# A decoder step's mixing tile in another order: an inverse without transpositions, its last level by substitution, and the next tile's scores and routing rows inside it

## What is computed

```python
A = jnp.where(strict, jnp.einsum('bhncd,bhnjd->bhncj', kb, k) * decay, 0.0)
sol = lax.linalg.triangular_solve(eye + A, rhs, left_side=True, lower=True, unit_diagonal=True)
u, w = sol[..., :dv], sol[..., dv:]
qk = jnp.where(causal, jnp.einsum('bhncd,bhnjd->bhncj', q, k) * decay, 0.0)
...
    v_new = u_c - jnp.einsum('bhcd,bhde->bhce', w_c, S)
    o = jnp.einsum('bhcd,bhde->bhce', qg_c, S) + jnp.einsum('bhcj,bhje->bhce', qk_c, v_new)
    S = S * gl_c[..., None, None] + jnp.einsum('bhcd,bhce->bhde', kd_c, v_new)
```

## Time and profile before

| | us |
|---|---|
| median of 3 runs | 1625.16 (1621.95 to 1626.21) |
| the profiled execution | 1621.55 |
| its span, first to last instruction | 1619.7 |
| the mixing stage in it | 578.4 (406.6 to 985.0) |
| PE busy in the mixing stage | 528.5 |
| DVE, ACT, POOL busy in it | 405.6, 300.5, 109.7 |
| one tile, from o products to o products | 69.5 (742.9 to 812.4) |

### The profile page before, as it was taken

The page is one execution under the profiler, slowest core; times in us unless marked ns, Lnnn a source line. Parts: engine busy times, 40 slices in busy tenths (PEclk is TensorE's granted clock), DMA queues, the critical chain, the costliest instruction groups (busy, mean ns, idle before and its releaser), DMA issues. The chain is left out here.

```text
span 1619.7 us, 24144 instructions
## 1 busy us (share of the span) xinstructions
PE 1405.5 (87%) x9708; PEld 955.3 (59%) x9708; DVE 625.8 (39%) x1034; ACT 349.4 (22%) x730; POOL 215.9 (13%) x284
## 2 busy tenths in 40 slices
PE   6999999604899999999899983699999999839997
PEld 4679999502577686776868652445454545414443
DVE  2325452107554646546364525312121212124442
ACT  2322322101323323233232310011111111111111
POOL 0000000001302113021221200122222121100000
PEclk9999999855988988898887976799999999969999
DMA  5212322243202112021120106489999999633320
GB/s 178 85 40 79 104 85 86 27 143 103 83 8 76 40 44 82 8 76 31 54 82 9 40 4 240 164 307 348 339 352 338 360 342 341 243 126 110 111 71 27
DMA packets 149127, 218.03 MB, mean 135 GB/s; under 512 B 12476, under 2 KB 123652, under 8 KB 144423
## 3 DMA queue, kind: packets, MB, share of 16 engines
q1 hardware_dynamic: 130862, 168.92, 31.3%
q0 software_dynamic: 9504, 25.77, 4.2%
q10 hardware_dynamic: 8681, 22.14, 3.8%
HBM read 178.91 MB, written 42.54 MB: 137 GB/s over the span
## 5 line engine op out<-in xcount | busy, mean ns | idle before, releaser
L1719 PE MATMUL psum<-experts 128*128 128x512 f32 x528 | 235.2, 599 | 2.6 <-DVE experts L1741 2.6
L626 PE MATMUL psum<-split_parts 128*128 128x344 f32 x1224 | 194.1, 321 | 0.0
L626 PEld LDWEIGHTS psum<-split_parts 128*128 128x128 f32 x1224 | 193.9, 188 | 0.1
L1719 PEld LDWEIGHTS psum<-experts 128*128 128x128 f32 x528 | 101.2, 192 | 130.4 <-issue 127.2
L2094 PE MATMUL psum<-experts 128*128 128x512 f32 x288 | 127.5, 601 | 3.9 <-DVE experts L2005 3.9
L1735 PE MATMUL psum<-experts 128*128 128x512 f32 x264 | 119.2, 594 | 1.5 <-ACTq L1772 1.0
L1756 DVE COPY experts<-psum 128x256 f32<-128x256 f32 x33 | 14.0, 425 | 274.9 <-PE psum L1726 274.9
L1304 PE MATMUL psum<-decode_and_mix 128*128 128x512 f32 x256 | 114.9, 603 | 0.7 <-ACT decode_and_mix L1227 0.7
L1021 POOL TENSOR_TENSOR decode_and_mix<-decode_and_mix,lasting 128x16 f32<-128x16 f32 (+3 forms) x25 | 44.7, 1786 | 423.5 <-DVE decode_and_mix L1077 241.8
L2094 PEld LDWEIGHTS psum<-experts 128*128 128x128 f32 x288 | 55.6, 193 | 74.2 <-issue 69.9
L1304 PEld LDWEIGHTS psum<-decode_and_mix 128*128 128x128 f32 x256 | 48.2, 193 | 56.6 <-issue 55.2
(11 more groups left out here) (369 smaller groups left out, 1978.4 us busy)
## 6 DMA issues: line engine op xcount, KB each, us to landing
experts<-in_w_gate SPq DMA_DIRECT2D x33, 1024.0 KB, 5.9
experts<-in_w_up SPq DMA_DIRECT2D x33, 1024.0 KB, 10.7
experts<-in_w_down SPq DMA_DIRECT2D x33, 1024.0 KB, 12.3
project<-in_w_in SPq DMA_DIRECT2D x18, 512.0 KB, 4.9
experts<-ye_d SPq DMA_DIRECT2D x16, 512.0 KB, 5.3
conv_out_d<-project ACTq DMA_DIRECT2D x12, 512.0 KB, 3.1
decode_and_mix<-conv_out_d SPq DMA_DIRECT2D x8, 768.0 KB, 4.7
until_mixed<-in_x_prompt SPq DMA_DIRECT2D x8, 512.0 KB, 4.7
```

The source lines that it names most:

```text
L626: mm = nc.tensor.matmul(thirds(u)[:, b], w[:, u, k, :], x[:, k, b * TB:(b + 1) * TB], start=(i == 0 and k == 0), stop=(i == 2 and k == KD ...
L1719: mm = nc.tensor.matmul(bank(2 + s.v), xgT[s.v][:, k, :], wgu[s.u][:, k, :], start=(k == 0), stop=(k == KD - 1))
```

## The change

The tile is put into another order on all engines.

- The inverse no longer turns MT at each level. PE keeps M, the transpose of MT, summed up in PSUM: `added_product` adds was' Xs to it, beside PT = Xs' was for MT, and the masks of levels 1 to 5 carry the sign (so DVE adds). A level is X, then PT and M for each group; ACT copies X and M.
- The sixth level is gone. v of the low half is formed with the low inverse, w = ATo' vn is taken off the high half's right side (DVE), then v of the high half: `quarter` products of 64x64. ATo is multiplied by E_ and not by Eb.
- The next tile's scores stand in levels 4 and 5, and their bias, maximum and shift in DVE's level 4 and after level 5; its exponentials stand on ACT ahead of and after `squared`. The gates' sums and the turning of the next tile's tokens follow dS. The turning of the residual rows stands in level 3, and the router's product in two halves between v low, w and v high. The second half of the projection is cut in three, between the turnings, G, QK and values.
- POOL multiplies Eb and the output gate by its gain (szn), and makes gU for the next tile early. Masking of the first tile's scores is done for it alone. pT has two buffers, and PSUM banks are dealt out anew. All engines' loops over tiles are written out. The SBUF room of the stages (WORDS) grows from 50400 to 53200 words.

Core of the diff: SP, POOL, DVE, ACT and PE in turn; lines that begin with - of the old order are left out, except in two places.

```diff
-        c[:, C_LV + n * HD:C_LV + (n + 1) * HD] = (row // (2 * s) == near // (2 * s)) & (row // s < near // s)
+        c[:, C_LV + n * HD:C_LV + (n + 1) * HD] = ((row // (2 * s) == near // (2 * s)) & (row // s < near // s)) * (-1.0 if n else 1.0)
...
+                for t in range(NT):
+                    if t:
                         sp.wait_ge(S("tokv_ps"), t)
                         settle(sp)
+                        load_conv(sp, t * P)
                         sp.wait_ge(S("av_ps"), t)
+                        load_attention(sp, t, t * P)
+                    load_out(t)
+                    sp.wait_ge(S("szn"), t)
+                    sp.dma_start(szst, sz_d[t * P:(t + 1) * P, :]).then_inc(S("sz_in"), 16)
+                load_out(NT)
...
+                gates(0)
+                for t in range(NT):
+                    R = DEC if t == 0 else P
+                    if t:
                         rms_pow("o", r8, m8, NH, t - 1)
                     rms_pow("qk", r16, m16, 16, t)
+                    g.wait_ge(S("E"), t + 1)
+                    g.tensor_tensor(Eb, E_, bc(gb[:, t, 0:NH], P), ALU.mult).then_inc(S("Eb"), 1)
+                    if t < NT - 1:
+                        gates(t + 1)
+                    g.wait_ge(S("AT"), 3 * t + 2)
+                    for l in range(1, 4):
+                        masked(t, l)
                     rms_pow("x", rsx[0:R], msx[0:R], 1, t)
+                    for l in range(4, LV):
+                        masked(t, l)
+                    g.wait_ge(S("sz_in"), 16 * t + 16)
+                    if t:
+                        g.wait_ge(S("v_on"), t)
+                    g.tensor_tensor(slots(szn), natural(szst), slots(bm(normB, NH)), ALU.mult).then_inc(S("szn"), 1)
...
                 def gated_out(t):
                     v.wait_ge(S("r_o"), t + 1)
-                    V.tensor_tensor(o_, o_, bc(r8, HD), ALU.mult).then_inc(S("v_on"), 1)
                     v.wait_ge(S("v_on"), t + 1)
-                    V.tensor_tensor(natural(vn.rearrange("p h d -> p (h d)")), slots(o_), slots(r_), ALU.mult).then_inc(S("og"), 1)
...
+                    for l in range(1, LV):
                         for g in range(2):
...
+                            v.wait_ge(S(f"PT{g}_ps"), (LV - 1) * t + l)
+                            V.tensor_tensor(MT[l % 2][:, hs], MT[(l - 1) % 2][:, hs], PT_ps(g), ALU.add).then_inc(S(f"MT{g}"), 1)
+                        if l == 1:
+                            mean_square(t, R)
...
                             V.tensor_tensor(r_, vtok, tmp, ALU.subtract).then_inc(S("r"), 1)
+                        if l == 2:
+                            normed(t, R)
+                            V.tensor_tensor(slots(tmq), kqS_ps[:, :, 1], slots(bc(egam, HD)), ALU.mult).then_inc(S("v_qS"), 1)
...
+                        if l == 3:
+                            gain(t, R)
+                        if l == 4 and more:
+                            biased(t + 1, 0)
+                            maximum(t + 1, 0)
+                            shift(t + 1, 0)
+                    if more:
+                        biased(t + 1, 1)
+                        maximum(t + 1, 1)
                     for g in range(2):
...
+                        v.wait_ge(S(f"v{g}_ps"), 2 * t + 1)
+                        V.tensor_tensor(vn[LOW, hs], v_ps(g)[LOW], bc(gb[LOW, t, hs], HD), ALU.mult).then_inc(S(f"vn{g}"), 1)
+                    if more:
+                        shift(t + 1, 1)
+                    v.wait_ge(S("r"), t + 1)
+                    for g in range(2):
...
+                        v.wait_ge(S(f"w{g}_ps"), t + 1)
+                        V.tensor_tensor(r_[HIGH, hs], r_[HIGH, hs], w_ps(g)[HIGH], ALU.subtract).then_inc(S(f"r1{g}"), 1)
+                    logits(t, R)
+                    for g in range(2):
...
+                        v.wait_ge(S(f"v{g}_ps"), 2 * t + 2)
+                        V.tensor_tensor(vn[HIGH, hs], v_ps(g)[HIGH], bc(gb[HIGH, t, hs], HD), ALU.mult).then_inc(S(f"vn{g}"), 1)
...
+                def tile(t):
+                    R, more = DEC if t == 0 else P, t < NT - 1
+                    act.wait_ge(S("tok_ps"), t + 1)
+                    A.activation(sq, tok_ps, ACT.Square).then_inc(S("sq"), 1)
+                    act.wait_ge(S("tokv_ps"), t + 1)
+                    act.wait_ge(S("r"), t)
+                    A.activation(slots(vtok), natural(tokv_ps), ACT.Copy).then_inc(S("vtok"), 1)
+                    if t:
                         mix_rows(t - 1)
...
+                    for l in range(LV):
+                        if l > 0:
...
+                                act.wait_ge(S(f"X{g}_ps"), (LV - 1) * t + l)
+                                A.activation(Xs[:, 4 * g:4 * g + 4], X_ps(g), ACT.Copy).then_inc(S(f"X{g}"), 1)
+                        if l < LV - 1:
...
+                                act.wait_ge(S(f"M{g}_ps"), (LV - 1) * t + l + 1)
+                                A.activation(M_[:, 4 * g:4 * g + 4], M_ps(g), ACT.Copy).then_inc(S(f"M{g}"), 1)
+                        if l == 0:
+                            norm_rows(t, R)
+                        if l == 3:
+                            store_rows(t, R)
+                    if more:
+                        exps(t + 1, 0)
+                    squared(t)
+                    if more:
+                        exps(t + 1, 1)
...
+                def added_product(out, g, left, right, first=False):
+                    for h in range(4 * g, 4 * g + 4):
+                        for rows in (LOW, HIGH):
+                            mm = T.matmul(out[rows, h % 4, :], left(rows, h), right(rows, h), start=first and h == 4 * g, stop=True, skip_group_check=True)
+                    return mm
...
+                def quarter(out, g, left, right):
+                    for h in range(4 * g, 4 * g + 4):
+                        mm = T.matmul(out[:, h % 4, :], left[:, h, :], right[:, h, :], start=True, stop=True)
+                    return mm
...
+                def tile(t):
+                    R, more = DEC if t == 0 else P, t < NT - 1
+                    if t:
                         turn_out(t - 1)
                         pe.wait_ge(S("mixB"), t)
+                        pe.wait_ge(S("mixA"), t)
...
+                    else:
+                        pe.wait_ge(S("s1"), 2)
...
+                    project(t, 0, range(KD))
                     pe.wait_ge(S("qk"), t + 1)
                     pe.wait_ge(S("D"), t + 1)
                     pe.wait_ge(S("egam"), t + 1)
...
+                    turned_weights(t, 0)
+                    project(t, 1, range(5))
                     pe.wait_ge(S("qkT"), t + 1)
...
+                        mm = T.matmul(G_ps[:, s, :], kT, kT, start=True, stop=True)
                     mm.then_inc(S("G_ps"), 1)
...
+                    turned_weights(t, 1)
+                    pe.wait_ge(S("pT0"), t + 1)
...
+                        mm = T.matmul(QK_ps[:, s, :], qkT[half_of(h), 4 + h // 2, :], qkT[half_of(h), h // 2, :], start=True, stop=True)
                     mm.then_inc(S("QK_ps"), 1)
+                    project(t, 1, range(5, 6))
                     pe.wait_ge(S("pT1"), t + 1)
+                    values(t, 0)
+                    values(t, 1).then_inc(S("av_ps"), 1)
+                    project(t, 1, range(6, KD)).then_inc(S("proj_ps"), 1)
+                    for g in range(2):
+                        pe.wait_ge(S(f"MT{g}"), LV * t + 1)
+                        if g == 1:
                             pe.wait_ge(S("mixA"), t + 1)
+                        added_product(M_ps(g), g, lambda rows, h: MT[0][rows, h, :], lambda rows, h: ident[rows, rows], first=True).then_inc(S(f"M{g}_ps"), 1)
+                    for l in range(1, LV):
+                        was = MT[(l - 1) % 2]
+                        for g in range(2):
+                            pe.wait_ge(S(f"M{g}"), (LV - 1) * t + l)
+                            pe.wait_ge(S("Lo"), (LV - 1) * t + l)
+                            pe.wait_ge(S("AT"), 3 * t + 3)
+                            pe.wait_ge(S(f"MT{g}"), LV * t + l)
+                            inverse_product(X_ps(g), g, lambda rows, h: Lo[l][rows, h, :], lambda rows, h: M_[rows, h, :]).then_inc(S(f"X{g}_ps"), 1)
+                        if l == 1:
+                            pe.wait_ge(S("QK"), t + 1)
...
+                            mm.then_inc(S("kS_ps"), 1)
+                        if l == 3:
+                            turn_rows(t, R)
+                        if l == 4 and more:
+                            scores(t + 1, 0)
+                        if l == 5 and more:
+                            scores(t + 1, 1)
+                        for g in range(2):
+                            pe.wait_ge(S(f"X{g}"), (LV - 1) * t + l)
+                            pe.wait_ge(S(f"MT{g}"), LV * t + l)
+                            inverse_product(PT_ps(g), g, lambda rows, h: Xs[rows, h, :], lambda rows, h: was[rows, h, :]).then_inc(S(f"PT{g}_ps"), 1)
```

(21 more changed lines are left out.)

506 lines of the change are left out of this document (217 added, 289 removed).

## The result

The changed kernel takes **1580.5 us** (median of 4 runs, 1579.27 to 1584.67) against 1624.34 (4 runs): a ratio of 0.9735, 95% interval 0.9712 to 0.9758. That is 43.8 us faster; 27.4 were forecast. The time lies in the stated range of 1564 to 1621, but under the 1584 to 1612 that the forecast had as its own. In the profiled executions the span went from 1619.7 to 1577.2 us, 42.5 less.

What follows compares the result with a forecast made beforehand. A tile was bound by PE's queue plus its waits. Six tiles 22.8, last 7.1, first -3.2, end 0.7: 27.4 us off 1621.55 gives 1594.2, plus 3.6 to the median: 1598; range 1564 to 1621, its own 1584 to 1612.

Steps and rivals of the forecast that it cites:

- full clock throughout: Rival: routing between the quarters keeps the clock up; tile 60.0 us, whole kernel 1562 us; chance 0.17.
- S1: Tile from end of o to the projection: the chain, not PE, sets it; 7.9 us before and after.
- S2: Tile from projection to inverse: 25.8 us before, 21.5 summed at full clock, 22.4 with the low clock.
- S3: Tile from the inverse to level 5: levels of 3.0 against 3.54 us; 24.9 before, 22.1 summed, 22.2 in the tile.
- S4: Tile's tail, last level, v and o: 10.9 us before, 9.2 at full clock, 12.2 forecast with the low stretch.
- Clock: Whole tile: order alone worth 3.5 us, the rest clock; 60.0 at full clock, 64.7 with the remaining low stretch.
- first low stretch: Clock at 0.50 in the old tile's inverse, 777.9 to 784.7; should go with the wait ahead of it.
- second stretch: Clock at 0.50 from 805.2 into the next tile's scores; should stay, since one-quadrant products with waits remain.
- First tile, last tile, end: Mixing stage's edges: first tile 67.3 against 64.1 us, last tile 7.1 less, 0.7 less after it.
- Into the projection: Rival: the low stretch runs on through S1 into the projection, +2.6 us a tile, 1618 us; chance 0.10.
- DVE late: Rival: DVE late ahead of MT or vn, waits longer than summed, +2 us a tile, 1613 us; chance 0.10.
- The inverse at 1.2 GHz: Rival: the inverse's products run at half clock, 9.5 us more a tile, 1671 us; chance 0.08.

Runs made afterwards that it cites:

- dve_late2: Changed kernel, with VectorE forming vn of the low half before the next tile's bias and maximum, and logits in their own bank: 1566.5 us.
- order: Changed kernel with vn before bias and maximum (logits in own bank), gated output ahead of E_, and first tile's exponentials behind its square: 1556.3 us.
- order_sd: The order kernel with the next tile's second scores moved into the tail and two 512-column products that nothing reads: 1565.3 us.

## Why the prediction was right, and by how much it was off

The time fell into the range, and the named mechanism holds: the new order shortens PE's queue, the low stretch ahead of the inverse goes and the one at the o products stays. The size was 1.6 times the forecast, and the time lies outside the forecast's own 1584 to 1612, on the side of its rival *full clock throughout* (1562). By its steps:

- **S1** (7.9 forecast, 8.47): taking the scores out saved nothing, as said; the chain sets it. It is a little longer than summed, because at half clock the gate sums hold E_ and with it `gated_out`. At full clock it was mis-sized the other way: 7.2 summed, 6.35 in the run with dense products. The low clock thus costs 2.1 here, not 0.7. PE was to idle for about 2 us ahead of the projection; it idles for 0.36 and 0.69.
- **S2** (22.4, measured 21.18 in every tile): the wait for `gain` left and MT and q, k were in time, as costed. The 0.9 for a projection at half clock was wrong: the low stretch ends while the turnings run, and the projection is at 1.00 in each tile.
- **S3** (22.2 in the tile's sum, 22.1 in its own; measured 21.82): levels of 3.04 as summed. The gain from the missing turnings was put at 0.54 in four levels; by the run that puts them back it is 1.07 in S3 for all, since three of the levels hold other products as cover.
- **S4** (12.2, measured 11.38, 10.2 to 12.3): the low stretch is there, at the o products, as said. It was to take a routing half, the quarters and o (+3.0); v low and the first routing half kept 1.00 in every tile; of the six it began at w in two, at the second routing half in two and at v high in two. At full clock the 9.2 was too long: about 8.0, an estimate from 10.73 in the run with dense products less 2.7. The low clock then costs some 3.4, near the 3.0.
- **Clock.** "The first low stretch should go with its wait": it went from the six tiles, but the wait was half of the reason. The wait without the routing costs a dip in every second tile; the routing without the wait none. The first tile, with its other wait, still has a low stretch in the inverse. The second stretch was put down to one quadrant with waits between. The waits are not needed for it (dve_late2), and dense products in between remove it, so sparse work is the part that is shown; one quadrant alone is not.
- **First tile, last tile, end**: +3.25 (3.2), 59.3 (61.4), -0.8 (-0.7). The first agrees by luck. Its inverse took 26.15 where 22.2 were summed, with the wait and the low stretch shown above, and its tail 9.18 where 12.2 were. Nor are the exponentials, named as the cause, worth more than the 0.65 above. The 2.2 us ahead of the stage belong to the runs.

The mis-sized term is thus the tile, 64.7 for 62.85, and two errors partly cancel in it. By the estimates above its work at full clock is about 57.2 and not 60.0: 0.85 less in S1, 0.3 in S2, 0.4 in S3, 1.2 in S4. The clock costs some 5.6 and not 4.7: more in S1 and S4, nothing in S2. So what the tile gained is the order's; the clock costs no less than the 5.0 that it cost in the tile before by the prediction's estimate (68.5 against 63.5).

The rivals. *Full clock throughout* did not come, but its all-fast tile of 60.0 was still too long: about 57. *Into the projection* did not come: at 793.40 to 795.90 turnings with half of the time idle stand at 1.00, and so does the projection behind them in all six tiles. This trace speaks against the rule quoted there from the Trainium skill (TensorE: Matmul & The Clock Gate, "Part 4: PE-mode transpose") without settling it. In other runs single tiles have a low projection: dve_late2 (0.76 over the first half, S2 22.88), order (0.77, S2 22.77) and order_sd, where the clock is 1.00 up to the projection and 0.50 as it starts (656.98 to 660.40). *DVE late* was in part true: its two waits of 0.9 a tile were in the sum of S4, but not that the run without them would be 14 us faster. *The inverse at 1.2 GHz* did not come in this kernel, but is one wait and one sparse product away from it: the run with both has it in part of the levels, at 28.6 for S3, and is slower than the kernel before.

The three parts undone one by one cost 2.0, 1.7 and 2.0 to 7.3 us a tile. They are not expected to add up to the 5.6 that a tile gained, since each also moves the low stretch.

## What to carry to other kernels

Where TensorE's clock falls in a stretch, cost an edit by the stretch's next neighbours too: removing 0.9 us of waits came with 2.0, since less of what stood behind them lay in the low clock. Such a gain may be a matter of where the low stretch falls, and it can differ from tile to tile. Look for a wait with sparse products behind it; taking away the wait ended the long low stretch here, and taking away the sparse products left short dips. And before another engine's work for the next tile is put ahead of a product that the path waits for, see whether it fits behind.

## What was not expected of the hardware

- Products that nothing reads made the kernel 15.9 us faster (1564.6 against 1580.5): four of 128x128 by 512 columns in each tail kept the granted clock at 1.00. Without them the products of v high (64x64 on one quadrant) and o (128x128 by 64 columns), behind narrow ones, ran at 0.56 though PE was busy for 4.99 of 4.99 us.
- The same wait of 2.16 us ahead of the same products left the clock at 1.00 in one tile and at 0.76 in the next, in turn.
- With the 128x36 routing products behind such a wait, the products of four quadrants that followed stood at a mean of 0.57 over 16 us, though these hold 1.00 elsewhere.
